# Scaling x four tiles at once on two engines, with the norm's weight folded into the high and low halves

## The reference, cut to what matters

```python
def rmsnorm(x, g):
    xf = x.astype(F32)
    y = xf * lax.rsqrt(jnp.mean(xf * xf, axis=-1, keepdims=True) + EPS)
    return (y * g.astype(F32)).astype(x.dtype)

h = rmsnorm(x, norm_pre[l])
p = split_cols(h @ w_in[l])          # 2048 columns in, among them e_q and e_g
oe = mem_attend(p["e_q"], mem_k[l], mem_v[l])      # * silu(p["e_g"]), and four more branches
gate = jax.nn.sigmoid(h @ w_merge[l])
x = x + rmsnorm(merged @ w_out[l], norm_post[l])
```

## Time and profile before

| | |
|---|---|
| median of 3 runs | 1885.9 us (1884.36 to 1887.4) |
| the profiled execution's own time | 1883.8 us |
| its span | 1882.1 us |
| granted TensorE clock over the span | 0.998 of full |
| TensorE (PE) busy | 1863.4 us (99%) |
| VectorE (DVE) busy | 1244.5 us (66%) |
| ScalarE (ACT) busy | 904.2 us (48%) |
| GpSimd (POOL) busy | 431.8 us (23%) |

### The profile page before, as it was taken

The page is one execution under the profiler, slowest core; times in us unless marked ns, Lnnn a source line. Parts: engine busy times, 40 slices in busy tenths (PEclk is TensorE's granted clock), DMA queues, the critical chain, the costliest instruction groups (busy, mean ns, idle before and its releaser), DMA issues.

```text
span 1882.1 us, 39418 instructions
## 1 busy us (share of the span) xinstructions
PE 1863.4 (99%) x16550; PEld 1799.9 (96%) x16550; DVE 1244.5 (66%) x2222; ACT 904.2 (48%) x1329; POOL 431.8 (23%) x722
## 2 busy tenths in 40 slices
PE   7999999999999999999999999999999999999998
PEld 6999999999999999999999999999999999999986
DVE  8554569777766667665787887876555555544544
ACT  7533335554554544445565666664333333433433
POOL 5677878688800000000000000001000000000000
PEclk9999999999999999999999999999999999999999
DMA  6887765655554554535445555556554554655542
GB/s 243 310 279 251 243 240 192 194 171 176 178 199 161 178 193 141 199 135 206 154 162 172 181 169 162 168 170 210 195 170 159 190 170 135 206 192 168 190 180 85
DMA packets 92898, 351.95 MB, mean 187 GB/s; under 512 B 11921, under 2 KB 12065, under 8 KB 87985
## 3 DMA queue, kind: packets, MB, share of 16 engines
q1 hardware_dynamic: 76896, 280.53, 44.1%
q0 software_dynamic: 11792, 48.81, 7.4%
q10 hardware_dynamic: 4032, 20.09, 3.0%
HBM read 322.46 MB, written 26.92 MB: 186 GB/s over the span
## 4 chain that ended last, share of the span: by engine, by line
PE 96%; DVE 2%; ACT 1%; issue 0%; DMA 0%; SPq 0%; DVEq 0%; ACTq 0%
PE ps L1826 95%; DVE w_lo L1158 1%; DMA raw<-in_w 0%; PE ps L2158 0%; ACT g_t L660 0%; PE ps L2015 0%; DVE o_y L1164 0%; ACT w_hi L660 0%; DVE xc L1164 0%; DVE g_X L1158 0%; PE ps L2048 0%; SPq L389 0%; DVE norm L1161 0%; DVE norm L1203 0%; PE ps L1939 0%
## 5 line engine op out<-in xcount | busy, mean ns | idle before, releaser
L1826 PE MATMUL ps<-h_hi,w_hi 128*128 128x288 f32 x2960 | 882.2, 299 | 2.8 <-ACT h_hi L660 2.3
L1826 PE MATMUL ps<-h_hi,w_lo 128*128 128x288 f32 x2960 | 871.6, 295 | 0.0
L1826 PE MATMUL ps<-h_lo,w_hi 128*128 128x288 f32 x2960 | 866.1, 294 | 0.0
L1158 DVE TENSOR_TENSOR w_lo<-raw,w_hi 128x1024 fp32r<-128x1024 f32 x498 | 621.8, 1259 | 293.9 <-ACT w_hi L660 291.1
L660 ACT ACTIVATE w_hi<-raw 128x1024 fp32r<-128x1024 f32 x498 | 522.6, 1056 | 467.4 <-PE ps L1826 415.0
L1826 PEld LDWEIGHTS ps<-h_hi,w_hi 128*128 128x128 f32 x2960 | 555.2, 188 | 10.8 <-issue 8.3
L1826 PEld LDWEIGHTS ps<-h_hi,w_lo 128*128 128x128 f32 x2960 | 555.6, 188 | 1.2
L1826 PEld LDWEIGHTS ps<-h_lo,w_hi 128*128 128x128 f32 x2960 | 555.4, 188 | 0.0
L1826 PE MATMUL ps<-br_hi,w_hi 128*128 128x288 f32 x640 | 192.1, 300 | 0.0
L1826 PE MATMUL ps<-br_hi,w_lo 128*128 128x288 f32 x640 | 188.8, 295 | 0.0
L1826 PE MATMUL ps<-br_lo,w_hi 128*128 128x288 f32 x640 | 188.3, 294 | 0.0
(11 more groups left out here) (396 smaller groups left out, 2244.8 us busy)
## 6 DMA issues: line engine op xcount, KB each, us to landing
raw<-in_w SPq DMA_DIRECT2D x498, 512.0 KB, 4.1
w_out<-in_w SPq DMA_DIRECT2D x24, 512.0 KB, 5.5
w_scratch<-st_wide POOLq DMA_DIRECT2D x72, 128.0 KB, 3.7
a_w<-w_scratch POOLq DMA_DIRECT2D x8, 1152.0 KB, 7.7
acc<-in_kc ACTq DMA_DIRECT2D x8, 1024.0 KB, 7.4
vc<-in_vc ACTq DMA_DIRECT2D x8, 1024.0 KB, 6.1
c_S<-in_gla POOLq DMA_DIRECT2D x4, 1024.0 KB, 8.1
out_gla_s<-c_S POOLq DMA_DIRECT2D x4, 1024.0 KB, 5.2
```

Source lines behind the costliest of these rows:

```text
L1158: return dve.tensor_tensor(out, a, b, ALU.subtract)
L1826: return pe.matmul(out, a, b, start=start, stop=stop)
```

## The change

It does seven things.

- VectorE multiplies x by `rstd` alone, four tiles in one instruction, for tiles 0 to 7 (2 instructions of 128 x 1152); GpSimd does the same for tiles 8 to 15 (2 instructions), in its program between the level masks and the small masks.
- ScalarE rounds one tile at a time (16 instructions) and multiplies by the norm's weight on the way (`scale=` with a column).
- VectorE writes each tile of `h_lo` as x times weight minus `h_hi` (16 instructions of 128 x 288), and does so after the low halves of units 2 and 3.
- TensorE's loop with the low weights of eq 1 moves ahead of the loop with `h_lo`. Both eq 0 and eq 1 are now completed by the last loop: `units_done` gets 1 at its tile 7 and 3 at its end.
- TensorE waits for `h_hi` and `h_lo` tile by tile.
- `WARM` goes from 3 to 5.
- Semaphores are merged or dropped: `eps_ready` and `ones_ready` into `constants`, `a_square` into `a_theta`, `d_abs_lam` and `d_halved` into `d_lam`, and `copied`, for which nobody waited.

```diff
-WARM = 3
+WARM = 5
...
+            pool.wait_ge(S("rooted"), 1)
+            for q in (2, 3):
+                ks = slice(4 * q, 4 * q + 4)
+                tt(ALU.mult, acc[:, ks], acc[:, ks], rstd[:].unsqueeze(1).to_broadcast([P, 4, T])).then_inc(S("scaled_by_pool"), 1)
...
-            for n in range(8):
-                ks = slice(n * 2, n * 2 + 2)
-                act.wait_ge(S("normed"), 2 * n + 2)
-                f(h_hi[:, ks], acc[:, ks], ACT.Copy, "high")
-                if n == 1:
+            act.wait_ge(S("norms_landed"), 16)
+            for k in range(KT):
+                act.wait_ge(S("scaled" if k < 8 else "scaled_by_pool"), k // 4 % 2 + 1)
+                f(h_hi[:, k:k + 1], acc[:, k:k + 1], ACT.Copy, "high", scale=norm_cols[:, 0, k:k + 1])
+                if k == 3:
                     upto(3)
...
-            link(dve.reciprocal(rstd[:], sd[:]))
+            sg(dve.reciprocal(rstd[:], sd[:]), "rooted")
+            dve.wait_ge(S("rooted"), 1)
+            for q in (0, 1):
+                ks = slice(4 * q, 4 * q + 4)
+                sg(mul(acc[:, ks], acc[:, ks], rstd[:].unsqueeze(1).to_broadcast([P, 4, T])), "scaled")
+            upto(3)
             dve.wait_ge(S("norms_landed"), 16)
-
-            def normed(q):
-                for k in range(4 * q, 4 * q + 4):
-                    sg(stt(acc[:, k], acc[:, k], norm_cols[:, 0, k:k + 1], rstd[:], ALU.mult, ALU.mult), "normed")
-
-            def split(q):
-                ks = slice(q * 4, q * 4 + 4)
-                dve.wait_ge(S("high"), 2 * q + 2)
-                sg(sub(h_lo[:, ks], acc[:, ks], h_hi[:, ks].bitcast(F32)), "split")
-
-            for q in range(4):
-                normed(q)
-            for q in range(4):
-                split(q)
+            for k in range(KT):
+                dve.wait_ge(S("high"), k + 1)
+                if k >= 8:
+                    dve.wait_ge(S("scaled_by_pool"), k // 4 - 1)
+                sg(stt(h_lo[:, k:k + 1], acc[:, k:k + 1], norm_cols[:, 0, k:k + 1], h_hi[:, k:k + 1].bitcast(F32), ALU.mult, ALU.subtract),
+                   "split")
             upto(4)
...
-                if k % 2 == 0:
-                    pe.wait_ge(S("high"), k // 2 + 1)
+                pe.wait_ge(S("high"), k + 1)
                 mm(first, w_hi[:, k // UK, k % UK], h_hi[:, k], k == 0, False)
                 mm(first, w_lo[:, k // UK, k % UK], h_hi[:, k], False, False)
                 mm(second, w_hi[:, 2 + k // UK, k % UK], h_hi[:, k], k == 0, False)
             for k in range(KT):
-                if k % 4 == 0:
-                    pe.wait_ge(S("split"), k // 4 + 1)
-                mm(second, w_hi[:, 2 + k // UK, k % UK], h_lo[:, k], False, False)
-                ins = mm(first, w_hi[:, k // UK, k % UK], h_lo[:, k], False, k == KT - 1)
-                if k % UK == UK - 1:
-                    sg(ins, units_done)
-            for k in range(KT):
                 if k % UK == 0:
                     pe.wait_ge(lo_ready, 3 + k // UK)
-                ins = mm(second, w_lo[:, 2 + k // UK, k % UK], h_hi[:, k], False, k == KT - 1)
-                if k % UK == UK - 1:
-                    sg(ins, units_done)
+                mm(second, w_lo[:, 2 + k // UK, k % UK], h_hi[:, k], False, False)
+            for k in range(KT):
+                pe.wait_ge(S("split"), k + 1)
+                mm(second, w_hi[:, 2 + k // UK, k % UK], h_lo[:, k], False, k == KT - 1)
+                ins = mm(first, w_hi[:, k // UK, k % UK], h_lo[:, k], False, k == KT - 1)
+                if k == UK - 1:
+                    ins.then_inc(units_done, 1)
+            ins.then_inc(units_done, 3)
```

More of the change, by code:

```diff
@@ L428, in _ @@
             link(pool.memset(ones[:], 1.0))
-            pool.memset(eps[:], EPS).then_inc(S("eps_ready"), 1)
+            pool.memset(eps[:], EPS).then_inc(S("constants"), 1)
             link(pool.memset(half_pi[:], float(np.pi / 2)))
-            pool.memset(ident[:], 0.0).then_inc(S("ones_ready"), 1)
-            pool.wait_ge(S("ones_ready"), 1)
+            pool.memset(ident[:], 0.0).then_inc(S("constants"), 1)
+            pool.wait_ge(S("constants"), 2)
             link(pool.affine_select(out=ident[:], in_=ident[:], compare_op=ALU.not_equal, fill=1.0,
@@ L472, in _ @@
             link(tt(ALU.mult, st_n, li, li))
-            tt(ALU.add, st_den, st_den, st_n).then_inc(S("a_square"), 1)
-            pool.wait_ge(S("a_square"), 1)
+            tt(ALU.add, st_den, st_den, st_n).then_inc(S("a_theta"), 1)
+            pool.wait_ge(S("a_theta"), 1)
             pool.wait_ge(S("a_dt"), 1)
@@ L704, in half_gate @@
                 f(e_th[:], out_of(("eg", n)), ACT.Tanh, "e_th", scale=0.5)
-            act.wait_ge(S("eps_ready"), 1)
+            act.wait_ge(S("constants"), 1)
             f(sd[:, 0:1], eps[:], ACT.Sqrt, "norm_sd")
@@ L732, in _ @@
             query(1)
-            act.wait_ge(S("norms_landed"), 16)
             for k in range(8):
@@ L738, in _ @@
             half_gate(0)
-            act.wait_ge(S("split"), 4)
+            act.wait_ge(S("split"), KT)
             load(kc[:, 0], t["kc"][0, :, 0], "kc_landed")
@@ L746, in _ @@
             half_gate(1)
-            act.wait_ge(S("a_theta"), 1)
+            act.wait_ge(S("a_theta"), 2)
             f(st_mag, st_a, ACT.Exp, "a_trig")
@@ L756, in _ @@
                 if i == 1:
-                    act.wait_ge(S("d_abs_lam"), 1)
+                    act.wait_ge(S("d_lam"), 1)
                     f(d_sp[:, 0], d_sp[:, 1], ACT.Exp, "d_exp_lam", scale=-1.0)
@@ L765, in _ @@
                 if i == 0:
-                    act.wait_ge(S("split"), 4 + KT)
+                    act.wait_ge(S("split"), 2 * KT)
                     load(vc[:, 0], t["vc"][0, :, 0], "vc_landed")
@@ L806, in _ @@
                     wait_block(act, "dx", 0)
-                    f(d_xp[:, 3:3 + SEQ], ps[:, bank(("dx", 0)), 0:SEQ], ACT.Copy, "copied")
+                    act.activation(d_xp[:, 3:3 + SEQ], ps[:, bank(("dx", 0)), 0:SEQ], ACT.Copy)
                     f(d_xs[:, :, 3:3 + NT], by_seq(ps[:, bank(("dx", 0))]), ACT.Copy, frees(("dx", 0)))
@@ L830, in _ @@
                     wait_block(act, "dx", i)
-                    f(d_xp[:, 3:3 + SEQ], ps[:, bank(("dx", i)), 0:SEQ], ACT.Copy, "copied")
+                    act.activation(d_xp[:, 3:3 + SEQ], ps[:, bank(("dx", i)), 0:SEQ], ACT.Copy)
                     f(d_xs[:, :, 3:3 + NT], by_seq(ps[:, bank(("dx", i))]), ACT.Copy, frees(("dx", i)))
@@ L837, in _ @@
                 if i == 0:
-                    act.wait_ge(S("d_halved"), 1)
+                    act.wait_ge(S("d_lam"), 2)
                     wait_block(act, "dg", 0)
@@ L990, in _ @@
                 act.wait_ge(S("g_rstd"), i + 4)
-                f(g_t[:, 2], src, ACT.Copy, "copied")
+                act.activation(g_t[:, 2], src, ACT.Copy)
                 f(g_t[:, 0], src, ACT.Abs, frees(("hf", i)))
@@ L1002, in _ @@
                 act.wait_ge(S("b_kz"), i + 1)
-                f(g_k[:], g_k[:], ACT.Exp, "copied")
+                act.activation(g_k[:], g_k[:], ACT.Exp)
                 f(g_t[:, 1], g_t[:, 0], ACT.Exp, "b_em")
@@ L1227, in split_memory @@
             def split_memory(k):
-                dve.wait_ge(S("high"), 8 + k + 1)
+                dve.wait_ge(S("high"), KT + k + 1)
                 sg(stt(m_lo[:, k:k + 1], mem[:, k:k + 1], norm_cols[:, 2, k:k + 1], m_hi[:, k:k + 1].bitcast(F32), ALU.mult, ALU.subtract),
@@ L1254, in _ @@
             gated(1)
-            dve.wait_ge(S("a_square"), 1)
+            dve.wait_ge(S("a_theta"), 1)
             sg(dve.reciprocal(st_den, st_den), "a_inverse")
@@ L1284, in decay @@
                     link(ts(d_sp[:, 3], lam, 0.0, None, ALU.max))
-                    sg(add(d_sp[:, 1], d_sp[:, 2], d_sp[:, 3]), "d_abs_lam")
-                    sg(ts(d_sp[:, 5:7], d_cols[:, 5:7], 0.5, None, ALU.mult), "d_halved")
+                    sg(add(d_sp[:, 1], d_sp[:, 2], d_sp[:, 3]), "d_lam")
+                    sg(ts(d_sp[:, 5:7], d_cols[:, 5:7], 0.5, None, ALU.mult), "d_lam")
                 elif step == 1:
@@ L1858, in branch @@
                 project(("b" + x, n), *home(MERGES.index(x)))
-            pe.wait_ge(S("ones_ready"), 1)
+            pe.wait_ge(S("constants"), 2)
             for q, sums in enumerate(x_sums):
@@ L1907, in _ @@
                 for v in range(2):
-                    project(("ek", 2 * i + v), m_hi, m_lo, N_MEM, wait_x={k: 5 + k for k in range(KT)} if i + v == 0 else ())
+                    project(("ek", 2 * i + v), m_hi, m_lo, N_MEM, wait_x={k: KT + 1 + k for k in range(KT)} if i + v == 0 else ())
                 project(("ev", 2 * i), m_hi, m_lo, N_MEM)
```

2 lines of the change are left out of this document (1 added, 1 removed).

## The result

Over 22 runs each the changed kernel takes 1888.89 us (1887.01 to 1892.42) and the kernel before 1884.85 (1883.72 to 1888.11). The medians differ by 4.0 us; the ratio of the compared runs is 1.0018, 95% interval 1.0012 to 1.0023, and by it the change is slower by 3.4 us (2.3 to 4.3). That is a small loss, but one clear of zero. It lies within the 0.2% (3.8 us) that the prediction calls no difference, and the upper end of the interval lies beyond. The forecast had 1888.1 and +2.2. That the time was met so closely is partly luck: the loss was larger than forecast, and the median of the kernel before, 1885.9 over three runs, came down to 1884.85 over 22. The profiled execution of the changed kernel took 1887.01, the fastest of its 22, with a span of 1885.3, 3.2 above before.

The account below looks back on a forecast made before the run. TensorE, 99% busy, was bounded by eg 0's start at 33.18, with TensorE, VectorE and the bank near-equal. The bank wait moves it to 35.4: 1885.9 + 2.2 = 1888.1 us, 8-in-10 range 1885.5 to 1890.6.

Parts of the forecast that it names:

- First matmul, 18.57: TensorE's first real matmul, after one VectorE product and one ScalarE rounding: 18.57 against 18.37, 0.2 later.
- Loop one, end at 26.5: TensorE's first loop, paced by ScalarE's roundings: ends at 26.35, or near 26.5 with GpSimd's products blocking VectorE 1.9 each.
- The upper bound from the 512-wide product, 2.4: GpSimd's 1152-wide product blocks VectorE for at most a full 2.4 us, by the 128x512 product's 1.058 us.
- the collision at 71 us: At 71.23 a GpSimd 128x256 product blocks VectorE about 0.42 us; taken as 1.9 for 1152 columns.
- The other collision in the earlier trace: Two GpSimd products in a row (1.21) lengthen another VectorE subtraction to 2.35 us; cited as exclusion.
- The bank wait, from `units_done` through ScalarE's program: ScalarE copies eq 0 only 4.16 after 31.1; eg 0 starts at 35.4, 2.2 late; chance alone 0.42.
- Hidden work: GpSimd's masks at 33 to 34, VectorE's unit 4 low half at 34.4: later, but covered, costing nothing.
- The clock's rival: TensorE's clock falls after idling ahead of eg 0, costing 1.6 more: +3.8 us, 1889.7; chance 0.33.
- Whatever that start gains or loses stays to the end: TensorE's stream behind the start of eg 0 is gap-free, so any shift there reaches the kernel's end.
- The size: The whole kernel's forecast loss: +2.2 us, to 1888.1.
- The 8-in-10 range: The kernel's time lies between 1885.5 and 1890.6, taking in the falling clock and the no-loss case.

Follow-up runs that it names:

- d1: The changed kernel again, unchanged, for a second trace: mean clock 0.999, eg 0 started at 36.56.
- b1: The kernel before with only the order of the loops (and VectorE's low halves) changed: median 1887.26 us, ratio 1.0008.
- c1: The changed kernel, with ScalarE copying eq 0 out of its bank ahead of unit 5's high half: median 1887.23 us, ratio 1.0007.
- r1: The changed kernel with all four 1152-wide products on VectorE and eq 0 copied ahead of unit 5's high half: median 1886.43 us, ratio 1.0003.
- p1: The changed kernel, with VectorE waiting for both GpSimd products before the low halves of units 2 and 3: median 1889.16 us, ratio 1.0019.
- v1: The changed kernel with WARM = 9, four more warm-up products: median 1888.93 us, ratio 1.0022.
- f1: The kernel before with only the folding, all four x products on VectorE, loop order as before, WARM 5: 1885.65 us, ratio 1.0006.
- w2: The kernel before with WARM = 5 and nothing else: median 1884.75 us, ratio 1.0003.
- o1: The changed kernel with TensorE's two loops back in the old order, GpSimd keeping its products: median 1888.03 us, ratio 1.0014.

## Why the prediction was right, and where not

- **First matmul, 18.57.** Measured 18.58; roundings at 0.43 from 17.90, as stated. The two more warm-up products moved the end of those matmuls by 0.4 us (16.06 to 16.43) in this trace and by 0.9 in d1, not by the 1.5 stated, and that changed nothing.
- **Loop one, end at 26.5.** It ended at 27.70. This is the term that was mis-sized: GpSimd's product blocks VectorE for 2.5 us, not 1.9, and since the engines take turns, the second one ended at 25.3 and not 24.2. The upper bound from the 512-wide product, 2.4, was nearly the truth; the value taken from the collision at 71 us was not. The other collision in the earlier trace rows said so already: two products of 256 columns lengthen a low half by 2.35 - 1.21 = 1.14, 0.57 each, and 4.5 times that is 2.6.
- **The bank wait, from `units_done` through ScalarE's program.** The mechanism and each of its steps held: 4.16 us from the high half of unit 4 to the end of the copy, releaser `eq_own`. b1 shows it alone, c1 and r1 show that nothing else binds within the next 1.0 and 2.3 us. Predicted 35.4, measured 36.44: 1.1 of it from loop one, less 0.1 for a shorter step from the copy to TensorE.
- **Hidden work.** Masks at 33.4 (33 to 34 predicted, needed at 35.9), unit 4's low half at 35.3: later than the 34.4 stated, still covered. VectorE's low halves of x, which I had called covered, are 0.3 us from binding, as p1 shows.
- **The clock's rival.** Right in place, kind and price (1.5 against 1.6), and shown by v1's trace. How many of the 12 runs at a lower mean clock lost it there no run shows. Its weight was argued from the length of the idle time, 2.2 against 2.31, and length was no guide: the clock fell behind 1.71 in v1 and did not behind 3.07 in b1. Two places were missing: loop one (f1), and 310 us (r1).
- **"Whatever that start gains or loses stays to the end."** So it was in the profiled execution. In the experiments it was not: eg 0 was 0.98 earlier in c1 and its execution 0.4 longer, in part by longer waits for low halves near 230 and 310 us. The prediction gave such waits no term.
- **The size.** +2.2 was forecast; the trace has +3.3 at eg 0 and +3.2 in the span, the runs +3.4. The term behind that is the 1.9 us. The 8-in-10 range held the time, and that 1888.1 lies within 0.8 of 1888.89 owes 1 us to the lower median of the kernel before.

## What to carry to other kernels

Before a loop is moved, ask what its old place covered: here 16 matmuls hid the copy that frees a bank, and the copying engine had 3.7 us of other work queued ahead of it, from the middle of the last loop on. The products given to GpSimd beside VectorE instructions with two SBUF operands were no extra throughput here: the two engines took turns, the instructions of both got longer, and the queue behind each inherited it. Where two paths end within 0.3 us of each other, as here, shortening one is worth that gap and no more.

## What the runs showed of the hardware

- A GpSimd product of 128x1152 f32 takes 2.67 us alone (p1) and 3.65 against VectorE; VectorE's 1.2 us low half beside it takes 3.68. The Trainium skill's rule in "SBUF — State Buffer", section on the two sides of SBUF, of an exclusive lock for the whole instruction fits these numbers, turn by turn.
- TensorE's clock fell to 0.50 about 0.2, 0.3, 1.2 and 1.5 us after the matmuls had set in behind idle times of 2.31, 1.71, 2.50 and 2.49 us (before, v1, w2, f1), and within an idle time of 3.02 (r1). It stayed at 1.00 behind 2.15, 2.29 and 3.07 (changed kernel, o1, b1): the length of the gap alone doesn't tell. The low stretch lasted 3.4 us in before, w2 and v1, and 6.8 in f1, the last 5 of these with TensorE busy without a pause.
- ScalarE's rounding of 288 columns with a column scale starts every 0.43 us, so 16 take 6.9 us; TensorE's three matmuls per tile take 0.40 at full clock, and in the changed kernel's loop one they start every 0.43, behind the roundings. The 576-wide roundings of the kernel before, without a scale, start every 0.57 for two tiles.
